# Four edits to a three-layer float32 decoder kernel on TensorE: full-row products, a longer first product, halved last rows, and identity products in four pauses

## The chip, the cores and the metric

One NeuronCore of one Trainium2 chip runs the whole program. The metric is device time in microseconds, median of the runs. The profile is of one execution; its times are counted from the first instruction.

## The reference, cut to what matters

Three layers act on x (256 tokens x 1024), float32 throughout.

```python
# layer 0: NSA mixer (compressed, selected and window attention) + memory attention
o_c = einsum('bgrqn,bngd->bqgrd', p_c, vc_b)      # 15 compressed blocks; 12 heads of 64
# layer 1: RWKV7 mixer + memory attention
g = sigmoid(zg) @ g2                              # zg: 256 x 160, g2: 160 x 768
kk = kk / maximum(sqrt(sum(kk * kk)), 1e-12)      # per head
# each of the two layers:
x = x + concatenate([mix, cross]) @ w_o[i]
x = x + swiglu(rmsnorm(x, norm2[i]), w_ffn_in[i], w_ffn_out[i])     # hidden 2816
# layer 2: spatial gate + "forgetting" attention, 8 heads of 128
c = cumsum(log_sigmoid(f + b_f))
s = q @ k.T + c[..., None] - c[:, :, None, :]; p = softmax(causal(s)); y_b = p @ v
x = x + rmsnorm((sigmoid(g_a) * y_a + sigmoid(g_b) * y_b) @ w_out, mix_post_g)
h = rmsnorm(x, ffn_pre_g)
x = x + rmsnorm((silu(h @ w_gate) * (h @ w_up)) @ w_down, ffn_post_g)
```

## The kernel before

All order is written by hand; each engine has its own program, and semaphores tie them.

Weights. A list of weight slots (1 MB each: 1024 rows x 256 columns, or 2 x 128 rows x 1024 columns) streams through a ring of three; SP issues the loads. ACT copies a slot into a high part `w_hi` (L1687), DVE subtracts it into a low part `w_lo` (`low_piece`, L2173), in two pieces. Two split slots exist, so a slot is split once the unit two places earlier is done. `ahead(name)` splits up to two slots past `name`.

Products. Every dense float32 product is three: high x high, high x low, low x high (`product`, L845 to L847). A *unit* is 48 of these with 256 columns (`fm_unit` with the weights held, `tm_unit` with the activations held) and fills one PSUM bank; `row_unit` works with 512 columns into four banks. `ffn(tag)` has 22 units `in0` to `in21` and 11 row units; the three feed-forward layers are f0, f1 and f2. After `in0`, `spread_scale` puts a few 128-column products between.

Banks. `unit(name)` gives a unit the next bank in turn (three in the first layer, four later); `begin(name)` waits until that bank's last user is read; `unit_done` counts units in this order, so the list and PE's program must agree.

Places that the change touches:

- NSA attention (`sparse_attention`): step s issues scores of head pair s, transposes of pair s-1, half a dense unit (`fill`), values of pair s-1, perhaps the other half, then `small_units`. Step 10 ends with `compressed_values` (L1337): 48 rows of trace with 15 weight rows and 64 columns, in two token tiles of 24. DVE reads its banks oc0 to oc3 (L2419).
- RWKV layer: `decay_and_rate`, z5, `out_gate` (L1473 with 128 weight rows, L1474 with 32, in turn, 12 float32 products that stand as 24 rows in a trace), memory attention's first scores, z0, then `head_sums("kn")` (L1439), which waits for ACT's squares (L1933). After `z8` comes `wkv()`, which begins with transposes (`token_rows`, L1109), two banks at a time, read by ACT.
- RWKV's end: cross products 4 to 6 (L845), `head_sums("gv")` (L1439), cross product 7, wait for the reciprocal (L2714), `head_spread("gr")` (L1449, 12 weight rows), row units of wo1.
- Forgetting attention: `scores(n)` adds -c by a product of `sel` and `ccum` with 8 rows (L1014) to q k (L1010), for each of two token tiles; a dense unit, transposes (L1023) and values (L1036) follow. Eight heads.
- End of layer 2's mixer: `gb3`, `to_fm` (16 transposes, L962, each four after a DVE addition L2857), ACT and DVE split them (L1656, L2153), row units of wo2. `last_rows` does the last two row units by token tile: tile 0 entirely (`tile0_done`), then tile 1.
- `post_squares` (ACT) and `post_norm` (DVE): per token tile two squares with sums (L1755), a root, a reciprocal, then per half bank x root x gain (L2135) and + x (L2138). ACT and DVE split another weight slot between the tiles (`between`). It runs after wo2 and at the very end; SP sends each finished half to HBM.
- `residual_to_fm`: 16 transposes of x (L972), eight per token tile, each half after its addition.

## Time and profile before

| | |
|---|---|
| runs (3) | 1208.3, 1209.39 and 2830.56 us, median 1209.39 us |
| profiled execution | 1207.98 us, span 1205.9 us |
| PE busy | 1157.0 us (96%), 9846 matmul rows |
| DVE, ACT busy | 759.1 us (63%), 602.9 us (50%) |
| mean granted TensorE clock | 0.985 |
| data read from HBM | 181.77 MB, 152 GB/s |

A float32 product with 128x128 weights stands in the trace as two matmul rows (of the split dense products, as one). A row's length holds its latency; what a row costs in a stream is the distance between two starts.

### The profile page before, as it was taken

To read this page: it belongs to the slowest core of one execution; us is meant where nothing else is said; L and a number is where in the kernel's file an instruction comes from. 1 tells how busy PE (TensorE), PEld (TensorE's weight loads), DVE (VectorE), ACT (ScalarE), POOL (GpSimd) and SP (SyncE) were. 2 spreads that over 40 slices of the span, in tenths; PEclk is the share of its full clock that TensorE was granted. 3 is DMA by queue.
4 is the path that set the end of the run, shared out by engine and by line. 5 is a ranking of instruction groups with operands and counts; after the bars stand their busy time and mean duration, and the time that the engine had idled before them with its cause. 6 is when DMAs were issued, how large, how long until landed. Compare 5 with 4: busy or idle time off the path is not lost.

```text
span 1205.9 us, 23192 instructions
## 1 busy us (share of the span) xinstructions
PE 1157.0 (96%) x9846; PEld 1067.5 (89%) x9846; DVE 759.1 (63%) x1291; ACT 602.9 (50%) x1029; POOL 31.9 (3%) x46
## 2 busy tenths in 40 slices
PE   6999889999999999899899999999999998999997
PEld 6999778999988978897699998899999987999985
DVE  5575646666645668766667674466754566666744
ACT  4666555444534673434345453354367745454533
POOL 0000000000000010330000000000000000000000
PEclk9999899999999998999899999999999999999999
DMA  9842225766654532001487665545654344676651
GB/s 283 242 134 92 71 71 150 220 185 179 199 182 157 175 106 105 2 4 50 127 221 216 186 201 190 194 141 177 183 166 122 124 140 129 187 205 183 205 182 63
DMA packets 218913, 185.35 MB, mean 154 GB/s; under 512 B 11266, under 2 KB 204048, under 8 KB 218684
## 3 DMA queue, kind: packets, MB, share of 16 engines
q1 hardware_dynamic: 217226, 181.50, 50.2%
q8 instruction: 78, 1.28, 0.4%
q0 software_dynamic: 384, 1.05, 0.4%
q10 hardware_dynamic: 1202, 1.34, 0.4%
q14 instruction: 23, 0.19, 0.0%
HBM read 181.77 MB, written 1.05 MB: 152 GB/s over the span
## 4 chain that ended last, share of the span: by engine, by line
PE 86%; DVE 8%; ACT 3%; DMA 1%; issue 1%; SPq 0%; ACTq 0%; DVEq 0%
PE bank L845 24%; PE bank L847 23%; PE bank L846 23%; DVE w_lo L2173 2%; PE bank L1376 1%; PE bank L1148 1%; PE bank L1159 1%; DMA ring<-in_w_ffn_in 1%; ACT w_hi L1687 1%; PE bank L1010 1%; PE bank L1352 1%; PE bank L1360 1%; PE bank L1014 1%; PE bank L972 1%; PE bank L1277 1%
## 5 line engine op out<-in xcount | busy, mean ns | idle before, releaser
L2173 DVE TENSOR_TENSOR w_lo<-ring,w_hi 128x1024 fp32r<-128x1024 f32 (+2 forms) x332 | 380.2, 1187 | 243.0 <-ACT w_hi L1687 242.8
L1687 ACT ACTIVATE w_hi<-ring 128x1024 fp32r<-128x1024 f32 (+2 forms) x332 | 324.1, 1027 | 395.6 <-PE bank L847 379.8
L845 PE MATMUL bank<-act_pair,w_hi 128*128 128x256 f32 (+1 forms) x1512 | 425.8, 282 | 6.1 <-issue 3.7
L846 PE MATMUL bank<-act_pair,w_hi 128*128 128x256 f32 (+1 forms) x1512 | 421.7, 279 | 0.0
L847 PE MATMUL bank<-act_pair,w_lo 128*128 128x256 f32 (+1 forms) x1512 | 421.6, 279 | 0.0
L845 PEld LDWEIGHTS bank<-act_pair,w_hi 128*128 128x128 f32 (+1 forms) x1512 | 284.1, 188 | 10.4 <-issue 8.1
L847 PEld LDWEIGHTS bank<-act_pair,w_lo 128*128 128x128 f32 (+1 forms) x1512 | 285.7, 189 | 0.3
L846 PEld LDWEIGHTS bank<-act_pair,w_hi 128*128 128x128 f32 (+1 forms) x1512 | 284.4, 188 | 0.2
L845 PE MATMUL bank<-w_hi,act_pair 128*128 128x256 f32 (+1 forms) x448 | 140.1, 313 | 5.1 <-DVE act_pair L2153 2.2
L847 PE MATMUL bank<-w_hi,act_pair 128*128 128x256 f32 (+1 forms) x448 | 137.2, 306 | 0.0
L846 PE MATMUL bank<-w_lo,act_pair 128*128 128x256 f32 (+1 forms) x448 | 137.1, 306 | 0.0
L845 PE MATMUL bank<-w_hi,hT_hi 128*128 128x512 f32 x264 | 102.8, 389 | 1.0 <-DVE w_lo L2173 1.0
L847 PE MATMUL bank<-w_hi,hT_lo 128*128 128x512 f32 x264 | 102.7, 389 | 0.0
L846 PE MATMUL bank<-w_lo,hT_hi 128*128 128x512 f32 x264 | 102.7, 389 | 0.0
L845 PEld LDWEIGHTS bank<-w_hi,act_pair 128*128 128x128 f32 x448 | 85.5, 191 | 14.4 <-issue 9.2
L2284 DVE TENSOR_TENSOR zshift<-bank,row_scale 128x512 f32<-128x512 f32 x66 | 45.6, 691 | 70.1 <-PE bank L847 70.0
L847 PEld LDWEIGHTS bank<-w_hi,act_pair 128*128 128x128 f32 x448 | 85.2, 190 | 4.1
L846 PEld LDWEIGHTS bank<-w_lo,act_pair 128*128 128x128 f32 x448 | 85.2, 190 | 4.0 <-issue 0.2
L845 PEld LDWEIGHTS bank<-w_hi,hT_hi 128*128 128x128 f32 x264 | 49.6, 188 | 11.5 <-issue 1.4
L847 PEld LDWEIGHTS bank<-w_hi,hT_lo 128*128 128x128 f32 x264 | 49.6, 188 | 10.2
L846 PEld LDWEIGHTS bank<-w_lo,hT_hi 128*128 128x128 f32 x264 | 49.6, 188 | 10.2
L1692 ACT ACTIVATE arena<-bank 128x256 f32<-128x256 f32 (+3 forms) x56 | 23.6, 447 | 25.5 <-PE bank L1148 15.5
(317 smaller groups left out, 1227.4 us busy)
## 6 DMA issues: line engine op xcount, KB each, us to landing
ring<-in_w_ffn_in SPq DMA_DIRECT2D x88, 512.0 KB, 5.2
ring<-in_w_in SPq DMA_DIRECT2D x28, 1024.0 KB, 5.3
ring<-in_w_ffn_out SPq DMA_DIRECT2D x22, 1024.0 KB, 4.9
ring<-in_rw_w_in SPq DMA_DIRECT2D x11, 1024.0 KB, 5.3
ring<-in_w_gate SPq DMA_DIRECT2D x22, 512.0 KB, 4.0
ring<-in_w_up SPq DMA_DIRECT2D x22, 512.0 KB, 5.2
ring<-in_w_down SPq DMA_DIRECT2D x11, 1024.0 KB, 4.9
ring<-in_w_o SPq DMA_DIRECT2D x8, 1024.0 KB, 4.8
```

What stands on the lines that cost most here:

```text
L845: pe.matmul(o, ahl[0], bhl[0], start=first, stop=False)
L846: pe.matmul(o, ahl[0], bhl[1], start=False, stop=False)
L847: return pe.matmul(o, ahl[1], bhl[0], start=False, stop=final)
L972: ins = pe.transpose(bank[base + k // 2][:, (k % 2) * S + qt * P:(k % 2) * S + (qt + 1) * P], x_tm[:, qt, k * P:(k + 1) * P], ident)
L1010: ins = pe.matmul(score_bank(n)[:, c:c + nk], q[:, qt * P:(qt + 1) * P], k[:, 0:nk], start=True, stop=(kind != "fox"))
L1014: ins = pe.matmul(score_bank(n)[:, c:c + nk], sel[0:NFH, i, :], ccum[0:NFH, 0:nk], start=False, stop=True)
L1148: ins = pe.matmul(bank_of(name)[half[q], a * CH:(a + 1) * CH], cms[(len(MERGES) * pr + li) % 2][gi][half[q], a, :], tms[gi][half[q], a, :] ...
L1159: ins = pe.matmul(bank_of(name)[half[q], a * CH:(a + 1) * CH], ems[gi][half[q], a, :], tt[pr][half[q], 4 * gi + a, :], start=True, stop=True)
L1687: ins = act.activation(tiles[0], raw, copy)
L1692: act.activation(dst, bank_of(name)[:, :] if src is None else src, func, scale=scale).then_inc(freed(own, name), 1)
L2173: ins = dve.tensor_tensor(tiles[1], raw, tiles[0], ALU.subtract)
L2284: dve.tensor_tensor(scaled[:, j % 2, :].rearrange("p (b t) -> p b t", b=2), two(f"{tag}_in{j}"), scaled_pair(), ALU.mult).then_inc(freed(o ...
```

## The change

1. The forget product uses all 128 rows: `sel` is built on 128 partitions, `ccum` is zeroed first. `out_gate` issues its six 128-row products first, then its six 32-row products.
2. `lead_unit` for units in1, in2 and in5 of each feed-forward layer: the unit's first product streams 288 columns instead of 256. The 32 extra columns fall into the bank's other half, which the unit overwrites later.
3. `last_rows` does tile 1 by halves and signals `half_done` between; `post_squares` and `post_norm` follow by halves; DVE multiplies the gain in before the root is there, and ends with one fused operation per half. The weight slot that was split between the tiles is now split in two pieces (between the halves, and at the end).
4. `idle_products(o, n)`: n products of the identity with itself, 128 columns, float32, into a bank that is free: 16 before `wkv()`; 14 before `head_sums("gv")` and 7 before `head_spread("gr")`; 8 before and 7 after `to_fm` for wo2; 14 between the token tiles and 7 after the transposes for f2.
5. `compressed_values` takes a list of token tiles: tile 0 now stands before the second half of dense unit kmem1 in step 10, tile 1 after it; the bank list follows (oc0, oc1, kmem1, oc2, oc3).

```diff
-    unit("kmem1", 1, proj["kmem1"])
-    for j in range(4):
-        unit(f"oc{j}")
+    for name in ("oc0", "oc1", "kmem1", "oc2", "oc3"):
+        unit(name, 1, proj.get(name))
...
+        def idle_products(o, n):
+
+            for _ in range(n):
+                pe.matmul(o[:, 0:P], ident, ident, start=True, stop=True)
...
+        LEAD = 32
+
+        def lead_product(o, o_long, ahl, bhl, b_long):
+
+            pe.matmul(o_long, ahl[0], b_long, start=True, stop=False)
+            pe.matmul(o, ahl[0], bhl[1], start=False, stop=False)
+            return pe.matmul(o, ahl[1], bhl[0], start=False, stop=False)
...
+                    if c == 0 and k == 0:
+                        lead_product(o, bank_of(name)[:, 0:long], held, moving, act[0].rearrange("p k n -> p (k n)")[:, 0:long])
+                    else:
+                        ins = product(o, held, moving, k == 0, k == KT - 1)
...
+            for half in range(2):
                 for j in pair:
...
+                        ins = last_product(j, a, 1, half)
+                    if half:
                         ins.then_inc(unit_done, 1)
...
+                if half == 0:
+                    ins.then_inc(sem("half_done"), 1)
...
-        def residual_to_fm(base, ready):
+        def residual_to_fm(base, ready, meanwhile=None):
...
             for qt in range(QT):
+                if meanwhile and qt:
+                    begin(meanwhile)
+                    idle_products(bank_of(meanwhile), 14)
...
+            if meanwhile:
+                idle_products(bank_of(meanwhile), 7)
             fm_ready()
...
-                    ins = pe.matmul(score_bank(n)[:, c:c + nk], sel[0:NFH, i, :], ccum[0:NFH, 0:nk],
+                    ins = pe.matmul(score_bank(n)[:, c:c + nk], sel[:, i, :], ccum[:, 0:nk],
...
-                fm_unit(f"{tag}_in{j}", fm_of[tag])
+                (lead_unit if j in (1, 2, 5) else fm_unit)(f"{tag}_in{j}", fm_of[tag])
...
+            begin("tr0_0_0")
+            idle_products(bank_of("tr0_0_0"), 16)
             pe.wait_ge(sem("wkv_ready"), 1)
...
             if s == 10:
-                compressed_values()
+                compressed_values((1,))
...
                 if s:
                     pair_values(s - 1)
+                if s == 10:
+                    compressed_values((0,))
                 if s < 7 or s in (8, 10, 12):
                     fill(s, 1)
...
+            for i in range(NT):
+                pe.matmul(bank_of(f"g2_{i // 2}")[:, i % 2 * S:(i % 2 + 1) * S], rw_g2[:, i * P:(i + 1) * P], lora[:, 1, :],
+                          start=(i % 2 == 0), stop=False)
+            for i in range(NT):
+                ins = pe.matmul(bank_of(f"g2_{i // 2}")[:, i % 2 * S:(i % 2 + 1) * S], rw_g2[0:32, MW + i * P:MW + (i + 1) * P],
+                                lora[0:32, 2, :], start=False, stop=(i % 2 == 1))
...
+        begin("gv")
+        idle_products(bank_of("gv"), 14)
         head_sums("gv", zt, "squares_ready", 1)
         cross_product(7)
+        begin("gr_0")
+        idle_products(bank_of("gr_0"), 7)
         pe.wait_ge(sem("rstd_ready"), 1)
...
         tm_unit("gb2", fm_of["b2"]), tm_unit("gb3", fm_of["b2"])
+        pe.wait_ge(*evacuated("gb0"))
+        idle_products(bank_of("gb0"), 8)
         to_fm("tm_ready", 3, 1)
+        begin("wo2_0")
+        idle_products(bank_of("wo2_0"), 7)
         fm_ready()
...
-        residual_to_fm(4, lambda i: (sem("post_added"), i + 1))
+        residual_to_fm(4, lambda i: (sem("post_added"), i + 1), "f2_in0")
...
+                    if qt and half:
+                        if after:
+                            high_pieces(split_no[after], (0,))
+                        act.wait_ge(*filled(final))
...
+                    if qt and half and after:
+                        low_piece(split_no[after], 0)
+                    dve.wait_ge(sem("post_squared"), 4 * n + 2 * qt + half + 1)
+                    if half == 0:
+                        dve.tensor_scalar(total, first, 1.0 / D, EPS, ALU.mult, ALU.add).then_inc(tick(own), 1)
+                    else:
...
+                    dve.tensor_tensor(u_g[:, qt, c], bank_of(tag, 2 * qt + half)[:, :], gains[:, GAIN[gain], c],
+                                      ALU.mult).then_inc(freed(own, tag, 2 * qt + half), 1)
...
+                    dve.scalar_tensor_tensor(out=dst[:, qt, c], in0=u_g[:, qt, c], scalar=rms[:, r, qt:qt + 1], in1=base[:, qt, c],
+                                             op0=ALU.mult, op1=ALU.add).then_inc(tick(own, "post_added"), 1)
+            if after:
+                low_piece(split_no[after], 1)
...
-        dve.tensor_copy(sel[0:NFH], ident[0:NFH, 0:NFH].unsqueeze(2).to_broadcast((NFH, NFH, P))).then_inc(tick(own), 1)
+        dve.tensor_copy(sel, ident[:, 0:NFH].unsqueeze(2).to_broadcast((P, NFH, P))).then_inc(tick(own), 1)
+        dve.memset(ccum, 0.0).then_inc(tick(own), 1)
```

How instructions move, at three places (line numbers shift between the two files: L1337 is L1383, L1439 is L1487, L1449 is L1497, L845 is L849, L2138 has no heir).

PE, step 10 of the NSA attention, before: mem_hi and w_hi are the dense unit kmem1, L1337 is all of the compressed values.

```order
L1360 MATMUL bank<-cst,sbuf_p 128x128 x6
L1376 MATMUL bank<-arena,sbuf_pt 128x64 x6
L845 MATMUL bank<-mem_hi,w_hi 128x256
...
L847 MATMUL bank<-mem_hi,w_lo 128x256
L1337 MATMUL bank<-arena 128x64 x24
L1352 MATMUL bank<-arena 128x128 x2
```

And after:

```order
L1406 MATMUL bank<-cst,sbuf_p 128x128 x6
L1422 MATMUL bank<-arena,sbuf_pt 128x64 x6
L1383 MATMUL bank<-arena 128x64 x12
L849 MATMUL bank<-mem_hi,w_hi 128x256
...
L851 MATMUL bank<-mem_hi,w_lo 128x256
L1383 MATMUL bank<-arena 128x64 x12
L1398 MATMUL bank<-arena 128x128 x2
```

Half of the compressed values now stands ahead of the 24 dense products.

PE, the end of the RWKV mixer, before: L1439 are the head sums gv, L1449 the head spread.

```order
L847 MATMUL bank<-w_hi,act_pair 128x512
L1439 MATMUL bank<-arena,cst 12x256 x6
L845 MATMUL bank<-w_hi,act_pair 128x512
L846 MATMUL bank<-w_lo,act_pair 128x512
L847 MATMUL bank<-w_hi,act_pair 128x512
L1449 MATMUL bank<-zdelta,arena 128x256 x6
```

And after:

```order
L851 MATMUL bank<-w_hi,act_pair 128x512
L836 MATMUL bank<-cst 128x128 x14
L1487 MATMUL bank<-arena,cst 12x256 x6
L849 MATMUL bank<-w_hi,act_pair 128x512
L850 MATMUL bank<-w_lo,act_pair 128x512
L851 MATMUL bank<-w_hi,act_pair 128x512
L836 MATMUL bank<-cst 128x128 x7
L1497 MATMUL bank<-zdelta,arena 128x256 x6
```

Fourteen identity products (L836) stand ahead of the head sums, seven ahead of the head spread.

DVE, the last token tile of the program, before: L2127 to L2131 are the mean and the reciprocal.

```order
L2127 TENSOR_TENSOR small<-small 128x1
L2129 TENSOR_SCALAR small<-small 128x1
L2131 RECIPROCAL small<-small 128x1
L2135 SCALAR_TENSOR_TENSOR arena<-bank,small,arena 128x512
L2138 TENSOR_TENSOR rows_tm<-x_res,arena 128x512
L2135 SCALAR_TENSOR_TENSOR arena<-bank,small,arena 128x512
L2138 TENSOR_TENSOR rows_tm<-x_res,arena 128x512
```

And after:

```order
L2205 TENSOR_SCALAR small<-small 128x1
L2211 TENSOR_TENSOR arena<-bank,arena 128x512
L2208 SCALAR_TENSOR_TENSOR small<-small 128x1
L2211 TENSOR_TENSOR arena<-bank,arena 128x512
L2215 RECIPROCAL small<-small 128x1
L2219 SCALAR_TENSOR_TENSOR rows_tm<-arena,small,x_res 128x512 x2
```

Two of the four large operations now stand ahead of the reciprocal.

## Rows read from the trace of the kernel before

**Rows 1.** Page, part 4: the chain that ended last, by engine.
```profile
PE 86%; DVE 8%; ACT 3%; DMA 1%; issue 1%; SPq 0%; ACTq 0%; DVEq 0%
```
**Rows 2.** Stretches: us; busy (rows) of PE, PEld, DVE, ACT, POOL; PEclk, DMA, GB/s.
```profile
140.00:150.00 10.00, 9.15 (x78) 7.87 (x77) 5.56 (x17) 1.84 (x4) 0.00 (x0) 0.73 0.00 1
220.00:230.00 10.00, 10.00 (x88) 10.00 (x87) 6.32 (x10) 4.27 (x6) 0.00 (x0) 1.00 0.72 207
570.00:590.00 20.00, 17.61 (x56) 12.50 (x55) 12.66 (x18) 5.79 (x8) 0.00 (x0) 0.74 0.35 98
640.00:650.00 10.00, 10.00 (x91) 10.00 (x90) 7.21 (x10) 4.36 (x8) 0.00 (x0) 1.00 0.69 186
1010.00:1020.00 10.00, 5.92 (x36) 5.48 (x37) 9.54 (x20) 6.73 (x16) 0.00 (x0) 0.83 0.39 105
```
**Rows 3.** Timeline of PE, forgetting attention: start, us, line, tile, form, rows, [idle before].
```profile
908.55 0.83 PE L1036 MATMUL bank<-arena,sbuf_pt 128*128 128x128 f32 x6
909.22 0.39 PE L1010 MATMUL bank<-arena 128*128 128x128 f32 x2
909.53 0.48 PE L1014 MATMUL bank<-arena 8*128 8x128 f32 x2
...
911.20 0.39 PE L845 MATMUL bank<-w_hi,act_pair 128*128 128x256 f32 x1
```
**Rows 4.** Timeline of PE and ACT, output gate to head sums kn.
```profile
427.68 0.69 PE L1474 MATMUL bank<-arena 32*128 32x256 f32 x2
428.31 0.70 PE L1473 MATMUL bank<-arena 128*128 128x256 f32 x2
...
426.99 1.48 ACT L1927 ACTIVATE arena<-arena 128x1536 f32<-128x1536 f32 x1 [5.46 <-DVE arena L2584]
...
438.20 2.75 PE L1439 MATMUL bank<-arena,cst 128*12 128x256 f32 x12 [0.62 <-ACT arena L1933]
```
**Rows 5.** Timeline of PE, compressed values and the scores behind them.
```profile
141.12 1.86 PE L1337 MATMUL bank<-arena 15*128 15x64 f32 x24
143.67 2.49 PE L1337 MATMUL bank<-arena 15*128 15x64 f32 x24 [0.69 <-issue]
```
**Rows 6.** Timeline of PE at the start of wkv.
```profile
489.11 1.34 PE L1109 MATMUL bank<-cst,arena 128*128 128x128 f32 x6 [2.15 <-ACT arena L1692]
```
**Rows 7.** Timeline of PE, end of the RWKV mixer.
```profile
569.15 2.76 PE L1439 MATMUL bank<-arena,cst 128*12 128x256 f32 x12
574.79 5.48 PE L1449 MATMUL bank<-zdelta,arena 12*128 12x256 f32 x12 [1.99 <-DVE zdelta L2714]
580.68 0.79 PE L845 MATMUL bank<-w_hi,act_pair 128*128 128x512 f32 x1 [0.40 <-DVE act_pair L2709]
```
**Rows 8.** Timeline of PE, transposes ahead of wo2, with the dense products behind.
```profile
982.33 0.66 PE L962 MATMUL bank<-cst,rows_tm 128*128 128x128 f32 x4 [1.07 <-DVE rows_tm L2857]
983.93 0.47 PE L845 MATMUL bank<-w_hi,act_pair 128*128 128x512 f32 x1 [0.94 <-DVE act_pair L2153]
...
986.73 0.63 PE L846 MATMUL bank<-w_lo,act_pair 128*128 128x512 f32 x1
987.15 0.63 PE L847 MATMUL bank<-w_hi,act_pair 128*128 128x512 f32 x1
```
**Rows 9.** Timeline of PE, transposes ahead of f2.
```profile
1008.65 1.03 PE L972 MATMUL bank<-cst,x_res 128*128 128x128 f32 x8
1013.07 0.66 PE L972 MATMUL bank<-cst,x_res 128*128 128x128 f32 x4 [3.38 <-DVE x_res L2138]
...
1015.39 0.55 PE L845 MATMUL bank<-act_pair,w_hi 128*128 128x256 f32 x1 [0.28 <-issue]
```
**Rows 10.** Timeline of ACT and DVE, the last token tile.
```profile
1198.38 0.60 ACT L1755 ACTIVATE sbuf_p<-bank 128x512 f32<-128x512 f32 x1 [3.41 <-PE bank L847]
1199.10 0.60 ACT L1755 ACTIVATE sbuf_p<-bank 128x512 f32<-128x512 f32 x1
...
1202.81 0.69 DVE L2138 TENSOR_TENSOR rows_tm<-x_res,arena 128x512 f32<-128x512 f32 x1
```

More of the change, by code:

```diff
@@ L1322, in compressed_turns, with compressed_values @@
                 ins.then_inc(unit_done, 1)
-        def compressed_values():
+        def compressed_values(tiles):
             pe.wait_ge(*evacuated("vcb"))
-            for qt in range(QT):
+            for qt in tiles:
                 begin(f"oc{2 * qt}"), begin(f"oc{2 * qt + 1}")
@@ L1469, in out_gate @@
                 begin(f"g2_{j}")
[L1470 to L1475 removed]
+            for i in range(NT):
[4 more added lines that the diff above has]
+                                lora[0:32, 2, :], start=False, stop=(i % 2 == 1))
+                if i % 2:
+                    ins.then_inc(unit_done, 1)
         def bonus_sums():
@@ L1688, in split_to, with high_pieces @@
                     ins.then_inc(tick(own, "hi_ready"), 1)
+        def high_pieces(m, which):
+            assert m == split_at[0]
+            r, v = landed[split_names[m]]
+            act.wait_ge(slot_landed[r], v)
+            act.wait_ge(*filled(split_names[m - SPLITS]))
+            for i in which:
+                lo, hi = pieces(split_names[m])[i]
+                act.activation(w_hi[:, (m % SPLITS) * SLOT + lo:(m % SPLITS) * SLOT + hi],
+                               ring[:, r * SLOT + lo:r * SLOT + hi], copy).then_inc(tick(own, "hi_ready"), 1)
         def evac(name, dst, func=copy, scale=1.0, src=None):
@@ L2118, in scaled_pair, with post_norm @@
             return row_scale.unsqueeze(1).to_broadcast((P, 2, S))
-        def post_norm(n, tag, gain, base, dst, between=None):
+        def post_norm(n, tag, final, gain, base, dst, after=None):
             r = 7 + 2 * n
             for qt in range(QT):
-                if qt and between:
-                    ahead(between)
-                dve.wait_ge(sem("post_squared"), 4 * n + 2 * qt + 2)
-                dve.tensor_tensor(ssq[:, r, qt:qt + 1], half_sum[:, qt, 0:1], half_sum[:, qt, 1:2], ALU.add).then_inc(tick(own), 1)
+                total, first, second = ssq[:, r, qt:qt + 1], half_sum[:, qt, 0:1], half_sum[:, qt, 1:2]
+                for half in range(2):
+                    c = slice(half * 512, (half + 1) * 512)
+                    if qt and half and after:
[4 more added lines that the diff above has]
+                    else:
+                        dve.wait_ge(*summed)
+                        dve.scalar_tensor_tensor(out=total, in0=second, scalar=1.0 / D, in1=total,
+                                                 op0=ALU.mult, op1=ALU.add).then_inc(tick(own, "post_mean"), 1)
+                    summed = last(own)
+                    dve.tensor_tensor(u_g[:, qt, c], bank_of(tag, 2 * qt + half)[:, :], gains[:, GAIN[gain], c],
+                                      ALU.mult).then_inc(freed(own, tag, 2 * qt + half), 1)
+                dve.wait_ge(sem("post_root"), 2 * n + qt + 1)
                 dve.wait_ge(*last(own))
-                dve.tensor_scalar(ssq[:, r, qt:qt + 1], ssq[:, r, qt:qt + 1], 1.0 / D, EPS, ALU.mult, ALU.add).then_inc(tick(own, "post_mean"), 1)
-                dve.wait_ge(sem("post_root"), 2 * n + qt + 1)
                 dve.reciprocal(rms[:, r, qt:qt + 1], rms[:, r, qt:qt + 1]).then_inc(tick(own), 1)
```

67 lines of the change are left out of this document (36 added, 31 removed).

## Prediction, written before the changed kernel had run

> **What bounds the kernel now.** I read the page's chain of waits first: PE carries 86% of it, DVE 8%, ACT 3% [rows 1]. So a microsecond that PE works less is worth one, wherever it doesn't then wait for DVE or ACT; and an edit on PE must be read at its own place. I then cut the span into stretches [rows 2]. The reader is to see three things in them. First, the granted clock is 1.00 nearly everywhere, but 0.73 and 0.83 in two 10 us stretches and about 0.74 in one of 20 us; that is 5.4, 3.4 and 10.4 us at 1.2 instead of 2.4 GHz. Second, each of these falls comes when PE had little to do or only products with few weight rows before it: compressed values with 15 rows, a wait of 1.99 us for the reciprocal, one of 3.38 us for x. Third, two stretches with nothing but the same 256-column dense products at full clock hold 88 rows (f0) and 91 rows (f1): the same product is spaced in two ways. Last I read the timeline of PE at the places that the change touches [rows 3 to 9] and the tail [rows 10].
>
> All below is summed against the profiled execution, 1207.98 us (span 1205.9); the median of the runs is 1209.39, 1.4 above it.
>
> **Forget products on 128 rows.** For one head, from 909.22 to 911.20, eight rows take 1.98 us: four with 128 columns and four with 256, in turn 128 and 8 weight rows [rows 3]. Rows that follow each other on all 128 rows are 0.11 apart with 128 columns (six in 0.67 us, same group) and 0.22 to 0.23 with 256 columns (twelve in 2.75 us, the head sums in [rows 4]). Uniform, the eight would take 4 x 0.11 + 4 x 0.225 = 1.35 us, 0.63 less, and eight heads make **-5.0 us**. PE waits for nobody in this part by the chain; ACT, which splits weights, takes exponentials and reads banks, is late next. The added work (a zeroing of `ccum`, a copy on more partitions at the same width) stands on DVE between units whose waits PE does not feel. Bounds: 0, if the wider weights cost what the turns did, and -5.4.
>
> The Trainium skill (TensorE: Matmul & The Clock Gate, Why this matters for your kernels) says that a matmul with 32 weight rows takes the same time alone as one with 128, and that only tiles at work together gain. By that rule the widening gives nothing. The trace shows that it is the turn from one number of rows to the other that costs, 0.31 us where 0.22 stand elsewhere; I go by the rows, and keep the rule as a rival.
>
> **Output gate.** It alternates too: two 256-column rows are 0.63 us apart from the next two [rows 4], so 24 rows cost 7.5 us and grouped some 5.5. But PE next has scores and z0 (some 6.6 us) and then waits 0.62 us for ACT's squares, which hang on the scan, the exponentials that ACT began at 426.99 after waiting 5.46 us for DVE, and a weight split [rows 4]; none of that waits for the gate. PE would only wait 2.6 us there. I take **0**; the range is -0.6 to +1.7 (the clock falls behind the longer wait).
>
> **The long first product.** It is the least certain part. 10 us / 88 minus 10 us / 91 [rows 2] is 0.0037 us per product; units in1 to in21 of f0 hold 21 x 48 = 1008 products: 3.8 us. Nothing in such a stream changes its spacing; it seems to be drawn at an interruption. A first product with 32 more columns is such an interruption, three times per layer. If it leads into the short spacing, and leaves f1 and f2 there, f0 gains **-3.8**. Bounds: +6.0 (f0 stays, f1 and f2 lose 17 units x 48 x 0.0037 = 3.0 each) and -3.8. The nine extra stretches of 32 columns cost 9 x 0.11/4 = 0.25, less in truth since latency is in it: **+0.1**.
>
> **Compressed values split.** Now 24 rows take 1.86 us, a 0.69 us gap follows, then 24 rows take 2.49 at a falling clock, and the clock stays low for 5.4 us [rows 5, 2]. The gap is the bank of oc0, which DVE must read; with 24 dense products between, it has long been read: -0.7. If the halves of 1.9 us, apart, no longer bring the clock down, the 5.4 us at half speed return 2.7. ACT and DVE have little to do there (1.84 and 5.56 busy of 10, rows 2). **-3.4**; bounds 0 and -3.4.
>
> **Last rows and norm, end of the program.** T is the start of the first square after PE, 1198.38. Before: squares until 1199.82, means, root, reciprocal, then four operations of 0.69 to 0.75, the last ending at 1203.50 [rows 10]. After: the first half is squared and multiplied by the gain while PE does the second; behind PE stand one square (0.72), the mean (0.2), gain on the second half (0.69) with the root beside it, reciprocal (0.2), two fused operations (0.7 each) = 3.3 us instead of 5.1: **-1.8**, bounds -1.4 and -2.5. The output transfers follow the same way.
>
> **The same at wo2, with pause four.** Before, PE ends at 1008.65, transposes tile 0 (1.03), waits 3.38, begins the dense stream at 1015.39 [rows 9], at half clock for 3.4 us [rows 2]. After, x's second tile is whole at about +3.6 instead of +5.6. But 14 identity products stand in front of its transposes. One such product is two rows of 128 columns, 2 x 0.11 = 0.22 us: 3.1 us, from +1.0 to +4.1; transposes until +5.2; seven more (1.6) until +6.7. That is the old start, so the earlier norm is spent. What is left is the clock: 3.4 us of dense products at half speed, of which 16 products fit: **-1.4**. Bounds: -2.5 and +4 (below).
>
> **The other pauses.** Ahead of wkv: 16 x 0.22 = 3.6 us in front of transposes that were ready; behind these PE used to wait 2.15 for ACT [rows 6]. PE is 1.4 late, and gets back some 1.2 of a clock that fell there: **+0.2**. Ahead of gv: 14 products, 3.1 us, in front of head sums that waited for nothing, and everything up to the reciprocal hangs on those sums: +3.1. The seven ahead of the spread lie in the 1.99 us wait. The spread would take 2.8 instead of 5.48 and let DVE start 1.3 earlier; the dense products from 580.68 on, at half speed to about 585 (10.4 us after the fall near 574.7, rows 2), return 2.1 [rows 7]; but spread and the wait for DVE behind it can bring the clock down again, for which I give back 1.3: +3.1 - 3.4 + 1.3 = **+1.0**. Ahead of wo2: 15 products (3.3 us) against waits of 1.07 and 0.94 [rows 8]; PE starts 1.2 later, and eight products 0.42 apart instead of some 0.21 return 1.6: **-0.4**. Bounds for the three together: -3 and +6.
>
> **Sum**: -5.0 + 0 - 3.8 + 0.1 - 3.4 - 1.8 - 1.4 + 0.2 + 1.0 - 0.4 = -14.5. From 1207.98 that is 1193.5; the runs' median stands 1.4 higher, so **1195 us**.
>
> **Rivals.**
>
> *The long product does not move f0's spacing.* For it: nothing in the trace shows what a longer product does. Against: both spacings exist for the same instructions. Then 1195 + 3.8 = 1199.
>
> *The rule above holds and wide forget products gain nothing.* Against it stand [rows 3]. 1195 + 5.0 = 1200.
>
> *The clock falls all the same behind the compressed values or in a pause.* For it: head spreads with 12 rows and transposes are left as they are. Each fall costs 1.4 to 2.7; two of them: 1195 + 4 = 1199.
>
> *Slower: the identity products stand in front of the work at half clock.* All 73 cost 73 x 0.22 = 16 us at full clock, 32 at half; the pauses that they fill are 2.15 + 1.99 + 1.07 + 0.94 + 3.38 = 9.5 us. At full clock the overrun of 6.5 us is in my terms; at half clock it is 22.5, 16 more: 1195 + 16 = 1211, slower than before. It decides from the point where the clock has fallen before the first identity product of a pause begins; against it, PE comes from dense products in three of four places.
>
> *The long product puts f1 and f2 into the wide spacing*: 3.8 + 6.0 more, 1205.
>
> **How the numbers follow.** Forecast 0.40 (1195), spacing stays 0.22, falls remain 0.15, rule 0.08, f1 and f2 wide 0.08, half clock 0.03, others 0.04. The range is 1189 to 1204: down by a further 6 for spacings elsewhere, in the other dense streams, and a smaller price of the pauses, up past the three rivals at about 1200 and one of them twice. What a measurement of this kernel can tell from no change is about 2%, 24 us: below 1185 is faster, above 1233.6 slower. My cases lie between: faster 0.06, same 0.92, slower 0.02.
>
> **What would show it.** In the changed profile, eight rows of a head's scores in 1.4 us instead of 1.98; 91 rows in a 10 us stretch of f0; PEclk 1.00 at the compressed values; 3.3 us from the last square to the last DVE operation; a wait of over 2 us ahead of kn; head sums gv 3.1 us later behind the cross products. The forecast is wrong if the score rows stay 0.31 apart, if f1 or f2 hold 88 rows in 10 us, or if the clock falls to half behind the identity products.

## The result, and the profile after

The changed kernel takes 1195.69 us (median of 4 runs, 1195.16 to 1196.21), the kernel before 1208.85 us beside it (4 runs, 1206.42 to 2830.56): a ratio of 0.9909 with a 95% interval of 0.988 to 0.9938. The run of 2830.56 us here, and two of experiment four (2758.99 and 1295.47 us), lie far above all others and stay out of the ratios, which are estimates from the runs that are left and not quotients of the medians. By the bound of 2% that is no change; the interval lies below 1. The forecast was 1195. The profiled execution has a span of 1194.4 us, 11.5 less than before.

The changed kernel's page, part 4, answers to [rows 1]:

```profile
PE 87%; DVE 6%; ACT 3%; DMA 2%; issue 1%; SPq 0%; DVEq 0%; ACTq 0%
```

DVE has lost 2 points of the chain. By the chain's pieces (`--critical`) that is 27 us: 13 lie ahead of the values of step 9, where the chain now runs through loads, and 14 between kn and gm, where it now follows PE. So the share is not what the change saved, and a larger share of PE is here no sign of more useful work.

Stretches of the changed kernel, cut where [rows 2] were (us; busy and rows of PE, PEld, DVE, ACT, POOL; PEclk, DMA, GB/s):

```profile
140.00:150.00 10.00, 9.81 (x90) 8.93 (x89) 5.19 (x13) 2.52 (x9) 0.00 (x0) 0.83 0.11 44
220.00:230.00 10.00, 10.00 (x90) 10.00 (x90) 6.86 (x10) 5.24 (x8) 0.00 (x0) 1.00 0.77 213
566.00:586.00 20.00, 18.42 (x85) 13.72 (x85) 12.03 (x16) 4.31 (x6) 0.00 (x0) 0.83 0.25 71
640.00:650.00 10.00, 10.00 (x90) 10.00 (x90) 6.85 (x9) 5.25 (x8) 0.00 (x0) 1.00 0.76 211
1004.00:1014.00 10.00, 9.40 (x81) 9.21 (x80) 8.48 (x19) 7.06 (x13) 0.00 (x0) 1.00 0.47 126
```

f0 holds 90 rows where it held 88 (91 were forecast). The clock is full ahead of f2 (0.83 before). It is not at the compressed values (0.83) nor behind the head spread (0.83 over 20 us): there it fell in spite of the change, for 3.4 and 6.8 us.

PE's timeline. One head's forget scores [rows 3], then output gate to head sums kn [rows 4]:

```profile
904.48 0.39 PE L1054 MATMUL bank<-arena 128*128 128x128 f32 x2
904.70 0.39 PE L1058 MATMUL bank<-arena 128*128 128x128 f32 x2
904.92 0.60 PE L1054 MATMUL bank<-arena 128*128 128x256 f32 x2
905.36 0.59 PE L1058 MATMUL bank<-arena 128*128 128x256 f32 x2
905.60 0.47 PE L849 MATMUL bank<-w_hi,act_pair 128*128 128x256 f32 x1
...
423.95 1.13 PE L1054 MATMUL bank<-kmem,qmem 64*128 64x256 f32 x4
433.29 2.75 PE L1487 MATMUL bank<-arena,cst 128*12 128x256 f32 x12 [0.82 <-ACT arena L2007]
```

Read the starts: eight rows now take 1.12 us instead of 1.98. The scores behind the gate start at 423.95, 5.5 us after its first row (7.4 before), and kn still waits for ACT.

Compressed values [rows 5], start of wkv [rows 6], end of the RWKV mixer [rows 7]; L836 are the identity products, two rows each:

```profile
139.67 1.86 PE L1383 MATMUL bank<-arena 15*128 15x64 f32 x24
146.01 1.30 PE L1383 MATMUL bank<-arena 15*128 15x64 f32 x14
...
481.62 3.79 PE L836 MATMUL bank<-cst 128*128 128x128 f32 x32
485.25 0.82 PE L1153 MATMUL bank<-cst,arena 128*128 128x128 f32 x6
486.32 0.93 PE L1153 MATMUL bank<-cst,arena 128*128 128x128 f32 x6 [0.25 <-ACT arena L1761]
...
564.83 3.29 PE L836 MATMUL bank<-cst 128*128 128x128 f32 x28
568.04 2.76 PE L1487 MATMUL bank<-arena,cst 128*12 128x256 f32 x12
571.55 1.72 PE L836 MATMUL bank<-cst 128*128 128x128 f32 x14
573.68 3.46 PE L1497 MATMUL bank<-zdelta,arena 12*128 12x256 f32 x12 [0.41 <-DVE zdelta L2799]
578.32 0.79 PE L849 MATMUL bank<-w_hi,act_pair 128*128 128x512 f32 x1 [1.17 <-DVE act_pair L2794]
```

The 0.69 us gap between the halves is gone. Ahead of wkv the wait of 2.15 is 0.25, but 3.63 us of identity products stand before it. The clock no longer falls there; 10 us behind the last values ahead of wkv, PE only, before and after:

```profile
486.00:496.00 10.00, 7.46 (x120) 0.83 0.00 0
...
481.00:491.00 10.00, 9.08 (x149) 1.00 0.00 0
```

Ahead of the head spread only 0.41 is left of 1.99, while the 14 products ahead of gv filled no wait at all.

Ahead of wo2 [rows 8] and of f2 [rows 9], and ACT's and DVE's last token tile [rows 10]:

```profile
971.57 1.95 PE L836 MATMUL bank<-cst 128*128 128x128 f32 x16
973.35 1.91 PE L1001 MATMUL bank<-cst,rows_tm 128*128 128x128 f32 x16
...
999.72 1.03 PE L1014 MATMUL bank<-cst,x_res 128*128 128x128 f32 x8
1000.59 3.29 PE L836 MATMUL bank<-cst 128*128 128x128 f32 x28
1003.72 1.04 PE L1014 MATMUL bank<-cst,x_res 128*128 128x128 f32 x8
...
1188.76 0.60 ACT L1826 ACTIVATE sbuf_p<-bank 128x512 f32<-128x512 f32 x1 [2.03 <-PE bank L851]
...
1190.54 1.41 DVE L2219 SCALAR_TENSOR_TENSOR rows_tm<-arena,small,x_res 128x512 f32<-128x512 f32 x2
```

Every transpose finds its data there: no wait stands in these rows. At the end, 1188.76 to 1191.95 is 3.2 us from the last square to the last DVE operation (5.1 before).

I cut both timelines at the same instructions of PE; differences of two starts, in us:

| from the start of ... to that of ... | before | after | change |
|---|---|---|---|
| program → values of step 9 | 132.46 | 133.89 | +1.4, chance |
| → transposes for wo0 (compressed values) | 37.50 | 35.33 | -2.2 |
| → scale of f0 | 34.95 | 35.24 | +0.3, chance |
| → output gate (f0) | 218.48 | 214.03 | -4.5 |
| → kn (gate) | 14.80 | 14.80 | 0.0 |
| → gm (wkv) | 126.22 | 126.89 | +0.7 |
| → scale of f1 (gv, spread) | 44.67 | 46.56 | +1.9 |
| → first forget scores (f1) | 275.96 | 275.71 | -0.3 |
| → scale of f2 (forget attention, wo2, pause four) | 137.31 | 130.13 | -7.2 |
| → PE's last row (f2) | 175.59 | 175.75 | +0.2 |
| → end of the span | 7.95 | 6.07 | -1.9 |

gm are the sums behind wkv (`gm_0` and the banks after it), the last work ahead of gv. The two marked as chance hold a clock fall of 3.4 us each that the kernel before did not have there, and the first holds 0.4 us more of loading at the start.

### The profile page after: what moved, and what is told of

Same layout as the page of the kernel before. It is cut to its first block, busy times and chain, and to the rows that moved or that the text cites. A ratio compares the mean times of both kernels' runs of the same rounds, so it can differ in the third digit from the quotient of the medians.

```text
span 1194.4 us, 23500 instructions
## 1 busy us (share of the span) xinstructions
PE 1158.1 (97%) x9992; PEld 1079.9 (90%) x9992; DVE 758.2 (63%) x1292; ACT 603.2 (51%) x1029; POOL 32.0 (3%) x46
## 4 chain that ended last, share of the span: by engine, by line
PE 87%; DVE 6%; ACT 3%; DMA 2%; issue 1%; SPq 0%; DVEq 0%; ACTq 0%
PE bank L849 24%; PE bank L851 23%; PE bank L850 23%; DVE w_lo L2258 2%; PE bank L1422 1%; PE bank L836 1%; PE bank L1192 1%; PE bank L1203 1%; DMA rows_tm<-in_mem 1%; PE bank L1398 1%; DMA ring<-in_w_ffn_in 1%; PE bank L1406 1%; ACT w_hi L1745 1%; PE bank L1080 1%; PE bank L1054 1%
## 5 line engine op out<-in xcount | busy, mean ns | idle before, releaser
L2258 DVE TENSOR_TENSOR w_lo<-ring,w_hi 128x1024 fp32r<-128x1024 f32 (+2 forms) x332 | 380.3, 1187 | 235.8 <-ACT w_hi L1745 235.0
L849 PE MATMUL bank<-act_pair,w_hi 128*128 128x256 f32 (+1 forms) x1503 | 421.2, 280 | 5.3 <-issue 3.4
L850 PE MATMUL bank<-act_pair,w_hi 128*128 128x256 f32 (+1 forms) x1503 | 417.4, 278 | 0.0
L851 PE MATMUL bank<-act_pair,w_lo 128*128 128x256 f32 (+1 forms) x1503 | 417.4, 278 | 0.0
L849 PEld LDWEIGHTS bank<-act_pair,w_hi 128*128 128x128 f32 (+1 forms) x1503 | 282.2, 188 | 9.4 <-issue 7.0
L851 PEld LDWEIGHTS bank<-act_pair,w_lo 128*128 128x128 f32 (+1 forms) x1503 | 282.3, 188 | 0.2
L849 PE MATMUL bank<-w_hi,act_pair 128*128 128x256 f32 (+1 forms) x448 | 140.6, 314 | 4.0 <-DVE w_lo L2258 1.6
L849 PE MATMUL bank<-w_hi,hT_hi 128*128 128x512 f32 x264 | 102.8, 389 | 1.0 <-DVE w_lo L2258 1.0
L849 PEld LDWEIGHTS bank<-w_hi,act_pair 128*128 128x128 f32 x448 | 85.2, 190 | 10.5 <-issue 4.5
L849 PEld LDWEIGHTS bank<-w_hi,hT_hi 128*128 128x128 f32 x264 | 49.6, 188 | 11.6 <-issue 1.4
```

The costliest lines, as they stand in the source:

```text
L849: pe.matmul(o, ahl[0], bhl[0], start=first, stop=False)
L850: pe.matmul(o, ahl[0], bhl[1], start=False, stop=False)
L851: return pe.matmul(o, ahl[1], bhl[0], start=False, stop=final)
L2258: ins = dve.tensor_tensor(tiles[1], raw, tiles[0], ALU.subtract)
```

## The experiments

Twelve kernels in three groups; the kernels of a group ran on one chip, beside the kernel before (in the first group experiments one, two, four and eight, in the second three, six, nine and eleven, in the third five, seven, ten and twelve). The clock falls at other places from run to run, so I read medians together with the table's stretches, each in its own profile. Of each kernel one run was profiled.

**One: forget products narrow again.**

```diff
-sel[:, i, :], ccum[:, 0:nk]
+sel[0:NFH, i, :], ccum[0:NFH, 0:nk]
```

> The changed kernel, with the forget product back on 8 rows. My theory, that turning between 8 and 128 weight rows costs some 0.1 us per matmul row: the eight heads cost 5.0 to 5.6 us more, about 1201 us, and the score rows of a head take 1.98 us again. Rival, that rows cost what their columns cost and the gain between the two kernels' forgetting attention came from a shift of dense spacing: at most 1 us more, 1196 to 1197 us.

1202.61 us (10 runs; ratio to before 0.9945, 0.9924 to 0.9966). From the first forget scores to the scale of f2 135.98 us against 130.13: 5.85 more. Its timeline of PE, one head:

```profile
908.58 0.39 PE L1054 MATMUL bank<-arena 128*128 128x128 f32 x2
908.90 0.48 PE L1058 MATMUL bank<-arena 8*128 8x128 f32 x2
909.31 0.70 PE L1054 MATMUL bank<-arena 128*128 128x256 f32 x2
909.94 0.69 PE L1058 MATMUL bank<-arena 8*128 8x256 f32 x2
910.57 0.39 PE L849 MATMUL bank<-w_hi,act_pair 128*128 128x256 f32 x1
```

1.99 us for the eight rows again, and close to the time that my theory gave (about 1201). Few weight rows alone don't cost it: the twelve rows of the head spread, all with 12 weight rows and 256 columns, start 0.22 apart at full clock. So the turn between weights of 128 and of 8 rows is the cost; full rows take it away.

**Two and three: the longer product left out, and alone.** The second is the kernel before with only this edit.

```diff
-(lead_unit if j in (1, 2, 5) else fm_unit)(f"{tag}_in{j}", fm_of[tag])
+fm_unit(f"{tag}_in{j}", fm_of[tag])
```

> The changed kernel, with ordinary first products in units in1, in2 and in5. If the 32 extra columns set the short spacing: at least one of the three feed-forward layers has the wide spacing (88 instead of 91 matmul rows in 10 us), 3.8 us for each such layer, so 1199.5 to 1203 us. If f0 only drew the short spacing by chance: no layer need be wide, 1195 to 1196 us.

> The kernel before with the longer first product alone (units in1, in2, in5 of each feed-forward layer); nothing else of the change. Theory A (the longer product turns a stream spaced 117.6 ns into one spaced 113.5, whatever the draw was): 90 or 91 rows in 10 us in f0, f1 and f2 in every profile, about 3.8 us for each layer that would have been wide; against a before that scatters over 1200 to 1216 on this kind of chip the median falls by 4 to 6 us (ratio 0.995 to 0.997) and the runs lie within 4 us of each other. Theory B (the spacing is drawn at the start and the longer product only happened to go with a short draw in the runs so far): ratio 1.000, the runs scatter as those of before, and some layer of the profile holds 87 or 88 rows in 10 us behind the longer products.

Left out: 1202.47 us (10 runs from 1191.76 to 1209.40; ratio 0.9943, 0.9906 to 0.998). Alone: 1206.88 (12 runs from 1203.82 to 1212.11; ratio 0.9985, 0.9962 to 1.0007). Stretches of f0, f1 and f2, PE only, first left out, then alone:

```profile
220.00:230.00 10.00, 10.00 (x87) 1.00 0.65 176
640.00:650.00 10.00, 10.00 (x87) 1.00 0.85 242
1060.00:1070.00 10.00, 10.00 (x87) 1.00 0.77 210
```

```profile
220.00:230.00 10.00, 10.00 (x90) 1.00 0.78 212
...
1060.00:1070.00 10.00, 10.00 (x91) 1.00 0.67 181
```

Without it all three layers of the profile are wide: f0, f1 and f2 take 4.9, 3.8 and 4.4 us more than in the changed kernel (by the table's stretches). Yet the fastest run is 4 us below the changed kernel's median: I take it that the same binary ran with short layers then, and that a layer's spacing is drawn anew in each run. That is argued from the times; only one run of each kernel has a profile. The scatter shows it best once I take from each run's time what its lower clock may cost, (1 - mean clock) x 1200 us:

| | runs | lowest to highest, so corrected |
|---|---|---|
| before, first group | 23 | 1183.4 to 1196.9 |
| before, second group | 18 | 1183.3 to 1193.7 |
| longer product left out | 10 | 1178.9 to 1198.6 |
| longer product alone | 12 | 1182.5 to 1186.7 |
| forget narrow, longer product in | 10 | 1185.6 to 1189.5 |
| experiment nine, longer product in | 6 | 1176.8 to 1186.2 |

13.5, 10.4 and 19.7 us of scatter without it, 4.2 and 3.9 with it, and 5.6 or less in all other kernels that have it but that of experiment nine, which still scatters over 9. Its worth is the mean of a draw, not a fixed 3.8. Alone it moved the median by 2.0 us, an interval that reaches 1, where theory A had 4 to 6, though the corrected mean fell by 4.0 (1188.6 in its group to 1184.6). Left out, the time came where the theory of the short spacing had it.

**Four: the longer product in every 256-column unit.**

```diff
+                    if n == 256 and c == 0 and k == 0:
+                        lead_product(...)
...
+                    if n == 256 and qt == 0 and k == 0:
+                        lead_product(...)
```

> The changed kernel with a 288-column first product in every unit of 256 columns, not only in1, in2 and in5. If a longer first product always leads into the short spacing (0.1135 us) and keeps it, every dense stream gets it: in the changed kernel some 45 units elsewhere stand at 0.1176 us, 48 products each, 0.2 us per unit: 6 to 9 us less, 1187 to 1190 us. If it only draws anew: 1195 to 1198 us, with both spacings in the trace.

1197.95 us (median of 6 runs; ratio 0.9929, 0.9896 to 0.9962), not the 1187 to 1190 of a longer product that always works. f0, f1 and f2 are as short as with three per layer. In layer 2's projections eight longer products met the wide spacing in an uninterrupted stream; five left it wide. It is no cure everywhere, and 110 more of them (119 in all) bring nothing.

**Five: 264 columns instead of 288.**

```diff
-        LEAD = 32
+        LEAD = 8
```

> The changed kernel with a first product of 264 columns instead of 288 at the same nine places. Theory A (any lengthening of one product lets the stream fall into the short spacing): f0, f1 and f2 hold 90 or 91 rows in 10 us, and the runs lie within 4 us of each other once the clock is allowed for. Theory B (the extra length must make up the lag of the wide stream, and 8 columns are too few): the runs scatter over 10 us or more as without the longer product, and a layer that starts wide stays wide behind these products, 3.8 us each.

1199.1 us (7 runs; ratio 0.9938, 0.9911 to 0.9966), corrected 1181.1 to 1190.0, 9 us of scatter (no proof by itself: so much has the kernel of experiment nine, with 288 columns). Its f0 and f2, PE only, behind the second and behind the third of these products:

```profile
216.00:224.00 8.00, 8.00 (x70) 1.00 0.77 202
230.00:238.00 8.00, 8.00 (x73) 1.00 0.73 206
...
1024.00:1032.00 8.00, 8.00 (x70) 1.00 0.82 228
1040.00:1048.00 8.00, 8.00 (x73) 1.00 0.74 206
```

Neither theory holds as it stood. Behind the second the stream was wide in both layers (70 rows in 8 us), behind the third short (73). In f2 the second had even met a short stream and turned it wide; in f1 the second and the third turned a wide stream short. With 288 columns at these nine places no product turned a short stream of f0, f1 or f2 wide in any of ten profiles (all that have the longer product at these nine places alone). Of the wide streams that they met, the second of a layer turned five of five short (f0) and the third six of six (f1, where a late weight slot had made the stream wide). The first, which stands behind the scale's small products, was followed by a wide stream in five of ten f0. What the length has to do with it I haven't settled.

**Six: the compressed values whole again.**

```diff
-                if s == 10:
-                    compressed_values((0,))
...
-                compressed_values((1,))
+                compressed_values((0, 1))
```

> The changed kernel with the compressed values undone: both token tiles again behind the whole dense unit kmem1 in step 10. Theory A (the split removes the wait for the bank of oc0 and part of a clock fall): the stretch from the values of step 9 to the transposes for wo0 grows by 2.2 us (the ledger of the two profiles) to 3.4 us (the forecast), the gap of about 0.7 us between the two tiles is back, and the time is 2 to 3.5 us above the changed kernel's. Theory B (the clock falls there by chance of where its windows lie, with or without the split): only the gap of 0.7 us returns, and the time is 0.5 to 1 us above.

1198.3 us (7 runs; ratio 0.9925, 0.9898 to 0.9951), against 1197.94 for the changed kernel in the same group: the medians don't part them, and theory A's 2 to 3.5 us are not in them. They are in the stretch. Whole, it takes 37.4 to 37.5 us in three profiles, each with the gap and a fall of 6.8 us. Split, it takes 33.6 to 33.7 in seven profiles, and 35.2 to 36.7 in the four in which the clock fell there, for 3.4 us in three and 6.8 in one. The mean of the eleven is 34.4, 3.1 below whole. By the stretch theory A holds, with theory B's chance in four of eleven.

```profile
142.46 1.86 PE L1384 MATMUL bank<-arena 15*128 15x64 f32 x24
145.01 2.53 PE L1384 MATMUL bank<-arena 15*128 15x64 f32 x24 [0.69 <-issue]
```

**Seven: the gate in turn again.**

```diff
-            for i in range(NT):
-                pe.matmul(bank_of(f"g2_{i // 2}")[:, i % 2 * S:(i % 2 + 1) * S], rw_g2[:, i * P:(i + 1) * P], lora[:, 1, :],
...
+                for a in range(2):
+                    i = 2 * j + a
+                    o = bank_of(f"g2_{j}")[:, a * S:(a + 1) * S]
+                    pe.matmul(o, rw_g2[:, i * P:(i + 1) * P], lora[:, 1, :], start=True, stop=False)
+                    ins = pe.matmul(o, rw_g2[0:32, MW + i * P:MW + (i + 1) * P], lora[0:32, 2, :], start=False, stop=True)
```

> The changed kernel with the output gate issued as before: per bank 128 weight rows, 32, 128, 32. Theory A (the gate lies in PE's slack, since the sums kn wait for ACT's squares, whose chain does not hang on the gate): the gate's rows take 7.5 us instead of 5.5, the wait ahead of kn shrinks from about 2.6 us to 0.6, and from the first gate row to kn it takes 14.6 to 14.8 us as in every profile so far; time unchanged within 1 us. Theory B (grouping is on the path): that stretch grows to 16.6 us and the time by 2 us.

1194.76 us (4 runs; ratio 0.9894, 0.9869 to 0.9919): theory A. The gate's 24 rows take 7.4 us to the next scores, grouped 5.5, and gate to kn is 14.79 both ways. But the two microseconds saved are not idle in most profiles. A stretch of 9 us behind the gate, PE only, in turn (this kernel), grouped (changed kernel), and grouped without the 14 products ahead of gv:

```profile
422.00:431.00 9.00, 8.44 (x58) 1.00 0.39 116
```

```profile
424.00:433.00 9.00, 8.47 (x53) 0.81 0.37 117
```

```profile
424.00:433.00 9.00, 9.00 (x49) 0.63 0.38 117
```

In turn (three kernels) the clock is full there in each profile. Grouped, in eleven, it falls each time: in three as kn begins, behind a wait of 2.3 to 2.6 us, in eight within this stretch, where half clock then uses up that wait. Twice the fall lasted 6.8 us and kn came 0.6 late.

**Eight: no identity products at all.**

```diff
         def idle_products(o, n):
-            for _ in range(n):
-                pe.matmul(o[:, 0:P], ident, ident, start=True, stop=True)
+            return
```

> The changed kernel with none of the 73 identity products. My terms: wkv 0.2 and gv 1.0 to 1.8 us came back, the pauses ahead of wo2 and f2 cost 1.6 and 1.4 us of clock but give back 1.2 and 1.0 us of products that stood in the way. Sum about -1 us: 1194 to 1196 us. Rival, that identity products are what makes the change pay: 1 to 5 us more, with four falls of the granted clock in the pauses.

1195.27 us (4 runs; ratio 0.9885, 0.9841 to 0.9929), the changed kernel's time. Up to PE's last row the clock fell nine times instead of six. By stretch: kn to gm 127.5 (0.6 more than with them, at 13.6 us of half clock instead of 6.8), gm to f1 44.7 (1.9 less), first forget scores to f2 131.2 (1.0 more). Gain and loss cancel.

**Nine: without the 14 ahead of gv.**

```diff
-        begin("gv")
-        idle_products(bank_of("gv"), 14)
```

> The changed kernel without the 14 identity products ahead of the head sums gv; the 7 ahead of the head spread stay. Theory A (these 14 stand on the path and bring no clock back, since it fell at 575.8 all the same): from the sums gm to the scale of f1 1.8 to 3.1 us less, and the time 2 to 3 us below the changed kernel's. Theory B (they hold the clock up in part): the clock falls for 10 us instead of 6.8 behind the head spread, which takes 1.4 to 1.7 us of the 3.1 back; net -1.4 at most. Theory C (they pay for themselves, as the change means them to): the time is the changed kernel's or above.

1194.04 us (6 runs; ratio 0.9891, 0.9862 to 0.992), 3.9 below the changed kernel in the same group; the two intervals overlap. Its timeline at the spread:

```profile
566.96 1.72 PE L836 MATMUL bank<-cst 128*128 128x128 f32 x14
569.10 2.85 PE L1497 MATMUL bank<-zdelta,arena 12*128 12x256 f32 x12 [0.42 <-DVE zdelta L2797]
```

gm to f1 takes 43.0 instead of 46.6. The spread takes 2.85, at full clock, where the changed kernel's first profile had 3.46. That is not the doing of the missing 14: in six of nine profiles with them the spread takes 2.85 as well, and so it does in experiment three, without any identity product. Theory A, and somewhat more than it said. Theory B has it the wrong way round: the fall lasted 3.4 us without the 14 and 6.8 with them (6.8 again in the twelfth kernel, which lacks them too, so that this half is chance).

**Ten: the last rows and the norm whole again** at both places, with the identity products kept: `last_rows`, `post_squares` and `post_norm` are those of the kernel before.

```diff
-        post_norm(0, "wo2_0", "wo2_3", "mix_post_g_2", x_tm, x_tm, "f2_in0")
+        post_norm(0, "wo2_0", "mix_post_g_2", x_tm, x_tm, "wo2_2")
```

> The changed kernel with the last rows, the squares and the norm undone at both places (token tile 1 whole, four DVE operations behind the root); the identity products stay. Theory A (both places pay): from PE's last row to the end of the span 8.0 us instead of 6.1, and ahead of f2, from the transposes for wo2 to the scale of f2, about 41 us instead of 39.2: together 3.7 to 4 us above the changed kernel. Theory B (ahead of f2 the earlier norm is spent, because the 14 identity products stand in front of the transposes anyway): there at most 0.5 us more, 2 to 2.5 us in all.

1199.3 us (4 runs; ratio 0.9929, 0.9902 to 0.9957). Ahead of f2, from the timeline of PE:

```profile
1003.21 0.65 PE L1006 MATMUL bank<-cst,x_res 128*128 128x128 f32 x4 [0.24 <-DVE x_res L2199]
1004.60 0.66 PE L1006 MATMUL bank<-cst,x_res 128*128 128x128 f32 x4 [0.73 <-DVE x_res L2199]
```

Waits of 0.24 and 0.73, of which 0.46 us reach f2's scale. From PE's last row to the end of the span 8.0 us instead of 6.1. The medians of this group have no changed kernel beside them; by the stretches it is theory B: of the earlier norm 1.9 us come at the end and hardly 0.5 ahead of f2.

**Eleven: the changed kernel again**, unaltered.

> The changed kernel once more, unaltered, on the same chip as the others of this call, so that differences of 1 to 3 us can be read against it and not only through before. All theories: a ratio of 0.988 to 0.994 to before, runs within 2 us of 1195.7 us if the spacing is short in all three feed-forward layers of each run; a run 3.8 us above would be a layer that stayed wide.

1197.94 us (6 runs, 1195.27 to 1199.11; ratio 0.9915, 0.9888 to 0.9942), and no layer wide in its profile. Three of the six runs lie more than 2 us above 1195.7, up to 3.4, so the band of 2 us that I expected was too narrow. Compared over groups, a median of these kernels is good to some 2 us, no better.

**Twelve: identity products only as long as the pause.**

```diff
-            idle_products(bank_of("tr0_0_0"), 16)
+            idle_products(bank_of("tr0_0_0"), 9)
...
-        idle_products(bank_of("gv"), 14)
...
-        idle_products(bank_of("gb0"), 8)
+        idle_products(bank_of("gb0"), 4)
...
-        idle_products(bank_of("wo2_0"), 7)
+        idle_products(bank_of("wo2_0"), 4)
```

> A candidate for a better kernel: the changed kernel without the 14 identity products ahead of gv, with 9 instead of 16 ahead of wkv (2.0 us against a wait of 2.15 before), and 4 and 4 instead of 8 and 7 ahead of wo2 (0.9 us each against waits of 1.07 and 0.94). Theory A (an identity product is free as long as it fits into the pause, and costs 0.22 us beyond it): 3.5 us from gv, about 1.5 at wkv and 1.5 at wo2, so 5 to 6.5 us below the changed kernel, near 1190 us. Theory B (the shorter runs of identity products no longer keep the clock up behind the pauses): the clock falls there for 3.4 to 6.8 us more, and the gain over the kernel without the 14 alone is 0 or below.

1192.09 us (5 runs, 1187.44 to 1193.22; ratio 0.9862, 0.9836 to 0.9888): the best of all, 3.6 below the changed kernel's 1195.69 as medians, in ratio 0.9862 against 0.9909 and 0.9915. The intervals just touch (0.9888 and 0.988), so the order is likely and not certain. First forget scores to f2: 128.8 us against 130.1. The transposes come without a wait worth the name:

```profile
970.39 1.47 PE L1001 MATMUL bank<-cst,rows_tm 128*128 128x128 f32 x12
972.05 0.66 PE L1001 MATMUL bank<-cst,rows_tm 128*128 128x128 f32 x4 [0.18 <-DVE rows_tm L2941]
```

Theory A holds in kind (1192, not 1190): the clock stayed full behind the shorter groups ahead of wkv, wo2 and f2. It fell twice between the gate and wkv, as in the changed kernel, but long before the nine products.

## Why the prediction was right, point by point

The total came out (1195 against 1195.69), and most terms did; two were too favourable, and two clock falls elsewhere added 1.7. That the total agrees to 0.7 us is in part luck: the terms sum to -14.5 and the spans differ by 11.5, the 1.4 us by which the median stood above the profile before are not there after, and the same kernel once more took 1197.94.

| term | forecast | this pair | over the profiles |
|---|---|---|---|
| forget products on 128 rows | -5.0 | -5.6 | -5.6 to -5.9 |
| output gate | 0 | 0.0 | 0, twice +0.6 |
| longer product (with +0.1) | -3.7 | -4.5 | a draw, 3.8 to 4.9 per wide layer |
| compressed values split | -3.4 | -2.2 | -3.1 |
| last rows, end of the program | -1.8 | -1.9 | -1.9 |
| wo2, pause four, ahead of wo2 | -1.8 | -1.6 | -1.6 |
| ahead of wkv | +0.2 | +0.7 | +0.7 |
| gv and spread | +1.0 | +1.9 | +2.5 |

*Forget products.* Right: eight rows in 1.12 us. I had worked out 1.35; the four with 256 columns stand 0.17 apart, not the 0.225 that I took from the head sums. That would be 0.86 us a head; 0.70 to 0.73 arrive (5.6 and 5.85 over eight), since behind the rows the second dense product starts 0.30 after the first instead of 0.22. The rival by the Trainium skill (TensorE: Matmul & The Clock Gate, Why this matters for your kernels) falls with the first experiment: the widening was worth 5.85 us there. The page speaks of matmuls one by one; what was paid here is the turn between weights of different row counts.

*Gate.* Right in the sum, and incomplete in the mechanism. I expected a wait of over 2 us ahead of kn, and the profile shows 0.82: a clock fall right behind the grouped gate uses up the rest. I had it as a bound only.

*Longer product.* Right in kind. The step "if it leads into the short spacing" held, and the rivals "does not move f0" and "f1 and f2 go wide" are out. Mis-sized was what it is worth: I took one layer, as the profile had drawn it, and f1 and f2 as short. They are drawn as well, so a single profile can't price this edit. And 88 against 91 rows in 10 us gave me 3.7 ns a product; by their starts the products of f0 stand 117.8 ns apart before and 113.3 after, 4.5 ns, and 1008 of these make the 4.5 us of this pair.

*Compressed values.* -2.2 in this pair, because the clock fell at 142.3 for 3.4 us; eleven profiles give -3.1. The term was right as a mean, and the condition "if the halves no longer bring the clock down" held in seven of eleven. The rival "the clock falls all the same" thus came in part, here and behind the spread, at the prices that I had put on it.

*Last rows, wo2, pause four.* As forecast, the spent norm too: experiment ten puts 0.46 us on it ahead of f2. Without identity products the new norm gives 137.3 - 5.6 - 131.2 = 0.5 us there, and with them another 1.0.

*gv: a return that did not come.* I had +3.1 - 3.4 + 1.3. The overrun was exact: from gm to gv 7.86 us instead of 4.73. The spread and the dense products behind it begin 1.25 us sooner after its start, as I had said (4.64 instead of 5.89 us from one to the other). The step that failed is the rest, the 2.1 - 1.3 = 0.8 us that the dense products were to win back: from the first of them to f1's scale both kernels take 28.4 us. The clock fell all the same, at 575.8 instead of 574.7, and so the dense products stood at half clock for 4.3 us, 4.2 before. That makes +3.1 - 1.25 = +1.9. With the 21 products gm to f1 takes 46.9 us (mean of nine profiles), with none 44.4 (three, 43.8 to 44.7), with the seven alone 43.5 (two, 43.0 and 44.0). So the 14 don't pay; whether the seven do, by 0.9 us, two profiles don't show.

*Ahead of wkv: the second mis-sized term, by half a microsecond.* From the last values ahead of wkv to its first chunk scores it takes 5.67 us with the 16 products (ten profiles) and 4.0 to 4.4 without (three): the overrun of 1.4 that I had. And the fall is gone: 3.4 us in each of the three without, none in the ten with 16 or in the one with nine. But from the chunk scores to gm that gives back 0.75, not 1.2, so the 16 cost 0.7. Nine products cost nothing in the one profile that has them: from those values to gm 77.6 us, with none 78.3, with 16 78.9.

*Signs.* Of those that I had named, the score rows (1.12 us, even shorter than the 1.4), gv 3.1 us later and the last norm came; f0 holds 90 rows and not 91, and neither the full clock at the compressed values nor the wait of 2 us ahead of kn is in the profile. One sign of being wrong came too: behind the seven products of the spread the clock fell to half, as told above. The rival "slower, at half clock" never came up: no group of identity products began at half clock in the changed kernel's profile.

## What to carry to other kernels

Look for streams in which the number of weight rows alternates, and pad or group them: here it cost 0.1 us a row. Fill a pause with idle work only where the engine would wait, and only as long as the wait lasts; what exceeds it stands on the path at full price. And when runs of one binary scatter by 10 us, cut several profiles at the same instructions before you price an edit of 3 us: as far as its profiles show, this kernel's scatter came from a spacing that each layer draws anew and from where the clock falls, and one profile holds one draw of each.

## What the runs showed of the hardware that I had not expected

The same 256-column product has two stable spacings, and its own length goes with them. PE's groups by line, high x low products over the same 80 us of f0 (230 to 310), of the kernel before and of the changed one:

```profile
L847 PE MATMUL bank<-act_pair,w_lo 128*128 128x256 f32 x228 | 64.1, 281 | 0.0
```

```profile
L851 PE MATMUL bank<-act_pair,w_lo 128*128 128x256 f32 x236 | 65.1, 276 | 0.0
```

228 rows of 281 ns each stand against 236 of 276 ns. In fourteen profiles a stream went from one to the other only at an interruption or at a product of another length: 32 more columns, at the second and third place of the feed-forward layers, turned eleven of eleven wide streams short, in layer 2's projections three of eight, and 8 more columns went either way.

The grouped gate, less work for PE, was followed by a clock fall in eleven of eleven profiles, the gate in turn in none of three. And identity products kept the clock up where they filled a wait: ahead of wkv, wo2 and f2 it fell in all three profiles without them and in none of eleven with them. But 14 of them in front of work that waited for nothing did not save the clock 8 us later: it fell in all nine profiles with them.
